# Attention worked by pairs of heads, with products in alternating halves of the array and transposes in rounds

## What is computed

```python
def block_attention(q, k, v):
    ...
    def one(qblk):
        s = jnp.einsum('bkgqd,bksd->bkgqs', qblk, k).astype(jnp.float32) * scale
        p = jax.nn.softmax(s, axis=-1).astype(v.dtype)
        return jnp.einsum('bkgqs,bksd->bkgqd', p, v)
    o = lax.map(one, qb)
    return o.transpose(1, 0, 4, 2, 3, 5).reshape(b, L, H * hd)
```

## Time and profile before

| | |
|---|---|
| median of 3 runs | 2622.45 us (2621.61 to 2622.78) |
| profiled execution | 2621.94 us |
| its span in the trace | 2620.1 us |
| mean granted TensorE clock | 0.965 of full speed |
| PE busy | 2414.7 us (92%) |
| DVE busy | 1489.8 us (57%) |
| ACT busy | 802.6 us (31%) |
| attention loop (first L969 to last L994) | about 1812.8 to 2041.8 us |

### The profile page before, as it was taken

One profiled execution on the slowest core, in us unless ns is written; L12 is line 12 of the kernel. 1 busy time (PEld: TensorE's weight loads), 2 busy tenths in 40 slices (PEclk: granted clock), 3 DMA queues, 4 the chain that ended last, 5 costly groups with the idle time before them and its releaser, 6 DMA issues.

```text
span 2620.1 us, 35077 instructions
## 1 busy us (share of the span) xinstructions
PE 2414.7 (92%) x14569; PEld 2083.2 (80%) x14569; DVE 1489.8 (57%) x2298; ACT 802.6 (31%) x1429; POOL 229.0 (9%) x257
## 2 busy tenths in 40 slices
PE   5899889989998897979999999799999979999998
PEld 3768758878887886769899998687767769989997
DVE  3376571278226865556464555596666466446555
ACT  3423332200221044253122223533444352213222
POOL 0022040033003301010000000200000010000001
PEclk9999999999999998989999999898999989999999
DMA  7401105500450021313222222111000112212221
GB/s 294 145 25 61 65 21 217 201 9 1 169 185 17 1 81 56 105 41 97 65 73 73 73 65 81 55 57 45 1 1 1 41 57 73 65 57 89 77 77 41
DMA packets 43853, 193.57 MB, mean 74 GB/s; under 512 B 5009, under 2 KB 5009, under 8 KB 36913
## 3 DMA queue, kind: packets, MB, share of 16 engines
q1 hardware_dynamic: 41472, 178.10, 20.1%
q0 software_dynamic: 2224, 13.24, 1.4%
HBM read 183.72 MB, written 7.60 MB: 73 GB/s over the span
## 4 chain that ended last, share of the span: by engine, by line
PE 79%; DVE 14%; ACT 3%; issue 2%; DMA 1%; POOL 1%; SPq 0%; DVEq 0%; ACTq 0%; POOLq 0%
PE pg L797 27%; PE pg L593 15%; PE pg L835 15%; PE pg L969 4%; PE ps L744 3%; PE ps L994 3%; PE ps L982 2%; PE ps L567 1%; DVE att L1690 1%; DVE wk L1696 1%; DVE rtb L1443 1%; PE ps L687 1%; DMA ring<-in_wstream 1%; PE ps L691 1%; PE ps L708 1%
## 5 line engine op out<-in xcount | busy, mean ns | idle before, releaser
L797 PE MATMUL pg<-hh,xhi 128*128 128x320 f32 x992 | 312.1, 315 | 25.2 <-DVE hl L1528 25.2
L797 PE MATMUL pg<-hl,xhi 128*128 128x320 f32 x992 | 308.4, 311 | 0.0
L797 PE MATMUL pg<-hh,xlo 128*128 128x320 f32 x992 | 308.1, 311 | 0.0
L1417 DVE TENSOR_TENSOR wlo<-ring,whi 128x1024 fp32r<-128x1024 f32 x129 | 156.9, 1222 | 185.9 <-ACT whi L1030 185.7
L593 PE MATMUL pg<-hh,whi 128*128 128x320 f32 x976 | 239.2, 327 | 23.3 <-DVE hl L1449 10.9
L593 PE MATMUL pg<-hl,whi 128*128 128x320 f32 x976 | 225.6, 313 | 0.0
L593 PE MATMUL pg<-hh,wlo 128*128 128x320 f32 x976 | 225.1, 312 | 0.0
L593 PEld LDWEIGHTS pg<-hh,whi 128*128 128x128 f32 x976 | 165.5, 192 | 62.4 <-issue 51.3
L797 PE MATMUL pg<-hh,whi 128*128 128x320 f32 x640 | 201.5, 315 | 12.9 <-DVE hl L1528 12.9
L797 PEld LDWEIGHTS pg<-hh,xhi 128*128 128x128 f32 x992 | 189.1, 191 | 28.6 <-issue 17.5
L797 PE MATMUL pg<-hl,whi 128*128 128x320 f32 x640 | 199.3, 311 | 0.0
(11 more groups left out here) (296 smaller groups left out, 4762.2 us busy)
## 6 DMA issues: line engine op xcount, KB each, us to landing
ring<-in_wstream SPq DMA_DIRECT2D x231, 512.0 KB, 3.7
adaring<-in_wada SPq DMA_DIRECT2D x21, 1024.0 KB, 5.1
ybuf<-in_wada SPq DMA_DIRECT2D x21, 1024.0 KB, 4.9
adabig<-in_wada SPq DMA_DIRECT2D x6, 1024.0 KB, 17.5
xk<-in_x SPq DMA_DIRECT2D x1, 2560.0 KB, 9.9
yssd_scratch<-ybuf POOLq DMA_DIRECT2D x2, 1280.0 KB, 6.2
xk<-yssd_scratch POOLq DMA_DIRECT2D x1, 2560.0 KB, 10.7
xk<-in_x_tok POOLq DMA_DIRECT2D x1, 2560.0 KB, 9.0
```

What stands on the lines that cost most here:

```text
L797: last = nc.tensor.matmul(out[:, half], w[:, k * P:(k + 1) * P], a[:, k, half * HALF:(half + 1) * HALF], start=k == 0 and m == 0, stop=k = ...
L1417: V.tensor_tensor(lo, flat(ring[:, s % RING]), hi.bitcast(F32), ALU.subtract).then_inc(wlo_ready, 1)
```

## The change

The units become 40 pairs `(hp, b)` (`ATT_PAIRS`): an even and an odd head of one block, 32 full pairs and 8 prompt pairs, every fifth pair being one of the latter.

- Scores of a pair are four products in the order even 512, odd 128, odd 512, even 128 columns, in three banks, the middle one shared; before the last product PE waits on `sc_side` for the second one. Even pairs use three banks of `pg`, odd pairs three of `ps`. The fourth bank of `pg` takes the transposes, the fourth of `ps` the value products of both heads.
- The ten transposes of a full pair go in three rounds of 4, 4 and 2 blocks through that one bank. ACT copies rounds 0 and 1 (512 columns each), DVE copies round 2 (`att_rest`, 256 columns). Each round waits for the copy of the round before it.
- The value products alternate between the two heads, that is between the two column halves of the array. One DVE copy of 128x128 evacuates both.
- DVE takes both maxima in a row, then one negation for both, one reciprocal for both, and two normalizing products. ACT takes two exps per pair.
- `pt` moves to memory that it shares with `hh` and its neighbours; `pr` has four buffers.

In iteration `p` the orders are, PE: transposes `(p-1, round 0)`, scores `p+1`, transposes `(p-1, 1)`, values `p-2`, transposes `(p-1, 2)`. ACT: exp `(p, even)`, copy `(p-1, 0)`, exp `(p, odd)`, copy `(p-1, 1)`. DVE: prob `p-1`, rest `p-2`, max `p+1`, evac `p-2`.

```diff
-ATT_UNITS = [(h, b) for h in range(ATTN_HEADS) for b in range(TT)]
+ATT_PAIRS = [(hp, b) for hp in range(ATTN_HEADS // 2) for b in range(TT)]
+NPAIR = len(ATT_PAIRS)
+def att_rounds(p):
+    if ATT_PAIRS[p][1] == PROMPT_TT:
+        return [[(0, 0), (1, 0)]]
+    blocks = [(par, j) for par in range(2) for j in range(TT)]
+    return [blocks[0:4], blocks[4:8], blocks[8:10]]
+def att_count(p, k=0):
+    full = sum(len(att_rounds(q)) for q in range(p)) + k
+    late = sum(len(att_rounds(q)) == 3 for q in range(p)) + (k > 2)
+    return full, full - late, late
...
+        def scores(p, par):
+            three = (ps if p % 2 else pg)[:].rearrange("p a b -> p (a b)")
+            if ATT_PAIRS[p][1] == PROMPT_TT:
+                return three[:, 1024 * par:1024 * par + P]
+            return three[:, 896:1536] if par else three[:, 0:NT]
+        turn_bank = pg[:, 1, 512:1024]
...
+            def att_scores(p):
+                hp, b = ATT_PAIRS[p]
+                kv = 2 * hp // (ATTN_HEADS // KV_HEADS)
+                if p >= 2:
+                    pe.wait_ge(pe_exp, 2 * (p - 1))
+                def product(par, c0, c1, k0):
+                    r = HD * par
+                    return nc.tensor.matmul(scores(p, par)[:, c0:c1], aq[r:r + HD, hp, b * P:(b + 1) * P],
+                                            ak[r:r + HD, kv, k0:k0 + c1 - c0], start=True, stop=True)
...
+                product(0, 0, SAMPLE, 0)
+                product(1, 0, P, NT).then_inc(sc_side, 1)
+                product(1, P, NT, 0).then_inc(sc_ready, 1)
+                pe.wait_ge(sc_side, 1 + sum(x[1] != PROMPT_TT for x in ATT_PAIRS[:p]))
+                product(0, SAMPLE, NT, NT).then_inc(sc_ready, 1)
+            def att_turn(p, k):
+                rounds = att_rounds(p)
+                if k >= len(rounds):
+                    return
+                pe.wait_ge(pr_ready, 2 * p + rounds[k][-1][0] + 1)
+                _, by_act, by_dve = att_count(p, k)
+                if by_act:
+                    pe.wait_ge(pt_done, by_act)
+                if by_dve:
+                    pe.wait_ge(pt_rest, by_dve)
+                for i, (par, j) in enumerate(rounds[k]):
+                    last = nc.tensor.transpose(turn_bank[:, i * P:(i + 1) * P],
+                                               pr[:, 2 * (p % 2) + par, j * P:(j + 1) * P], cm[:, IDENT, :])
+                last.then_inc(pt_ready, 1)
+            def att_pv(p):
...
+                for j in range(n):
+                    for par in range(2):
+                        v = tiles[par][j]
+                        value = (cvt if v == TT else av[:, v])[:, kv * HD:(kv + 1) * HD]
+                        last = nc.tensor.matmul(ps[HD * par:HD * (par + 1), 3, 0:P], value, pt[:, p % 2, n * par + j, :],
+                                                start=j == 0, stop=j == n - 1, skip_group_check=True)
+            att_scores(0)
+            for p in range(NPAIR + 2):
+                if 1 <= p <= NPAIR:
+                    att_turn(p - 1, 0)
+                if p + 1 < NPAIR:
+                    att_scores(p + 1)
+                if 1 <= p <= NPAIR:
+                    att_turn(p - 1, 1)
+                if p >= 2:
+                    att_pv(p - 2)
+                if 1 <= p <= NPAIR:
+                    att_turn(p - 1, 2)
...
+            def att_exp(p, par):
+                n = P if ATT_PAIRS[p][1] == PROMPT_TT else NT
+                if par == 0:
+                    act.wait_ge(mx_ready, p + 1)
+                    if p >= 2:
+                        act.wait_ge(pt_ready, att_count(p - 1)[0])
...
+            def att_max(p):
+                dve.wait_ge(sc_ready, 2 * (p + 1))
+                for par in range(2):
+                    last = V.reduce_max(mxs[:, p % 2, 0, par:par + 1], scores(p, par), AX_X)
+                link(last)
+                V.tensor_scalar(mxs[:, p % 2, 1], mxs[:, p % 2, 0], -HD ** -0.5, None, ALU.mult).then_inc(mx_ready, 1)
+            def att_prob(p):
+                n = P if ATT_PAIRS[p][1] == PROMPT_TT else NT
+                dve.wait_ge(pe_exp, 2 * (p + 1))
+                link(V.reciprocal(mxs[:, p % 2, 3], mxs[:, p % 2, 2]))
+                for par in range(2):
+                    row = pr[:, 2 * (p % 2) + par, 0:n]
+                    V.tensor_scalar(row, row, mxs[:, p % 2, 3, par:par + 1], None, ALU.mult).then_inc(pr_ready, 1)
+            def att_rest(p):
+                if len(att_rounds(p)) < 3:
+                    return
+                dve.wait_ge(pt_ready, att_count(p, 2)[0] + 1)
+                src, dst = turned_blocks(p, 2)
+                V.tensor_copy(dst, src).then_inc(pt_rest, 1)
+            att_max(0)
+            for p in range(NPAIR + 2):
+                if 1 <= p <= NPAIR:
+                    att_prob(p - 1)
+                if p >= 2:
+                    att_rest(p - 2)
+                if p + 1 < NPAIR:
+                    att_max(p + 1)
+                if p >= 2:
+                    att_evac(p - 2)
```

More of the change, by code:

```diff
@@ L226, in hybrid_step @@
         wlo = sb("wlo", [P, 2, KT, P], F32R)
+        with ExitStack() as ph:
+            pt = sb("pt", [P, 2, 2 * TT, P], F32, ph)
         hh = sb("hh", [P, KT, NT], F32R)
@@ L470, in hybrid_step @@
         pt_done = sem("pt_done")
+        pt_rest = sem("pt_rest")
+        sc_side = sem("sc_side")
         ao_ready = sem("ao_ready")
@@ L955, in _ @@
                 pe.wait_ge(tile_free[b], freed(b, T_AOUT))
-            def keys(b):
-                if b == PROMPT_TT:
[L960 to L983, removed]
-                last.then_inc(pt_ready, 1)
@@ L986, in att_pv @@
[L986 to L1007, removed]
+            def att_scores(p):
[7 more added lines that the diff above has]
+                                            ak[r:r + HD, kv, k0:k0 + c1 - c0], start=True, stop=True)
+                if b == PROMPT_TT:
+                    for par in range(2):
+                        product(par, 0, P, SAMPLE).then_inc(sc_ready, 1)
+                    return
[4 more added lines that the diff above has]
+                product(0, SAMPLE, NT, NT).then_inc(sc_ready, 1)
@@ new lines, in att_pv @@
+            def att_pv(p):
+                hp, b = ATT_PAIRS[p]
+                kv = 2 * hp // (ATTN_HEADS // KV_HEADS)
+                tiles = [[PROMPT_TT]] * 2 if b == PROMPT_TT else [[0, 1, 2, 3, TT], [TT, 0, 1, 2, 3]]
+                n = len(tiles[0])
+                _, by_act, by_dve = att_count(p + 1)
+                pe.wait_ge(pt_done, by_act)
+                if by_dve:
+                    pe.wait_ge(pt_rest, by_dve)
+                if p:
+                    pe.wait_ge(ao_done, p)
+                for j in range(n):
[4 more added lines that the diff above has]
+                                                start=j == 0, stop=j == n - 1, skip_group_check=True)
+                        if j == n - 1:
+                            last.then_inc(ao_ready, 1)
@@ L1371, in _ @@
             nc.scalar.copy(tr_evac_k[1], ps[:, 1, :].rearrange("p (k t) -> p k t", k=KV_HEADS)[:, :, 0:HD]).then_inc(tr_done, 1)
[L1372 to L1394, removed]
+            def att_exp(p, par):
[4 more added lines that the diff above has]
+                        act.wait_ge(pt_ready, att_count(p - 1)[0])
+                nc.scalar.activation(pr[:, 2 * (p % 2) + par, 0:n], scores(p, par), ACT.Exp, scale=HD ** -0.5,
+                                     bias=mxs[:, p % 2, 1, par:par + 1],
+                                     accum_out=mxs[:, p % 2, 2, par:par + 1]).then_inc(pe_exp, 1)
@@ new lines, in att_copy @@
+            def att_copy(p, k):
+                if k >= len(att_rounds(p)):
+                    return
+                act.wait_ge(pt_ready, att_count(p, k)[0] + 1)
+                if p >= 2 and k == 0:
+                    act.wait_ge(ao_ready, 2 * (p - 1))
+                src, dst = turned_blocks(p, k)
+                nc.scalar.copy(dst, src).then_inc(pt_done, 1)
+            for p in range(NPAIR + 1):
+                if p < NPAIR:
+                    att_exp(p, 0)
+                if p:
+                    att_copy(p - 1, 0)
+                if p < NPAIR:
+                    att_exp(p, 1)
+                if p:
+                    att_copy(p - 1, 1)
@@ L1899, in _ @@
             dve.wait_ge(tr_done, 16)
[L1900 to L1913, removed]
```

29 lines of the change are left out of this document (12 added, 17 removed).

## The result

The changed kernel takes 2649.0 us (median of 4 runs, 2647.2 to 2650.8) against 2622.2 before: a ratio of 1.0102, 95% interval 1.0089 to 1.0115. It is 27 us slower where 13 were forecast. The profiled execution took 2650.8 us and has a span of 2649.0 us, 28.9 more than before (that the span equals the median is chance).

The account below looks back on a forecast made before the run. Attention was taken as bound by PE's own instructions, afterwards by a ring through DVE. Eight groups at 234 us, a third at half clock, plus 5 for ends and 3 for start: 242, 13 more than now, 2635 us; range 2606 to 2655.

Parts of the forecast that it names:

- What bounds the kernel now: Attention before the change: bound by PE's own instructions, PE busy for 228.99 of 229.00 us.
- PE's work after the change: Attention: column and row halves overlap, so PE's occupancy per full pair falls from 6.42 to 3.92 us.
- The ring through DVE: Attention turn: PE and DVE wait for each other through rest, transposes, scores, max; 5.96 us per full pair.
- the wait on `sc_side`, costed at nothing: Scores of a full pair: wait ends inside the odd 512-column product, costing nothing; 0.3 us without that cover.
- The forecast of 2635: Whole kernel: 2621.9 + 13 us, with a third of the attention stage at half clock.
- The sizes of the turn: Attention: PE and DVE steps of one full-pair turn at full clock, together 5.96 us against 6.42.
- the group of five: Attention: four full pairs and a prompt one, 26.1 us at full clock against 27.7 before.
- The clock: Attention stage: PE's waits make the granted clock fall, a third at half clock, mean 0.83.
- The rival in which it holds: Attention stage: clock stays up, the 5.96 us turn runs all the way, 2612 us (2604 to 2617); chance 0.27.
- The second rival, row halves in series: Scores: row halves not side by side, 2.34 us a pair; 2648, up to 2670 with falling clock; chance 0.13.
- The range: Whole kernel: 2606 to 2655 us, meant to hold 8 in 10.

Follow-up runs that it names:

- e1: The changed kernel with the odd head's 128-column score product issued first, ahead of the even 512-column one: 2634.2 us.
- e7: The changed kernel with a full pair's score products issued head by head, so row halves do not run side by side: 2742.2 us.
- e2: The changed kernel with PE's scores of pair p+1 issued ahead of transposes (p-1, 0) instead of behind them: 2594.8 us.
- e5: The changed kernel with all 32 full pairs first and the 8 prompt pairs last: 2633.7 us.
- e10: The changed kernel with the edits of both e4 and e1, fillers plus odd 128-column product first: 2615.4 us.
- e4: The changed kernel with five unread 128-column filler products per turn, issued where PE would wait for DVE: 2625.8 us.
- e6: The changed kernel with a pair's value products issued head by head instead of alternating column halves: 2666.7 us.

## Why the prediction was wrong

- **What bounds the kernel now, and PE's work after the change: right.** PE's busy time fell from 229 to 183 us. Column halves overlap as the earlier trace rows said, 1.29 us for 20 passes; row halves overlap too (1.28 us in e1), which no row had shown; e7 shows what they are worth.
- **The ring through DVE: right in place.** In the waits above PE waits for `att_rest` 32 times and DVE for scores, and e2 removes the ring and 54 us with it, some 24 of them by way of the clock. The way of the ring is half right. The prediction took it over DVE's maxima and had the value products end 0.17 us before their evacuation is due (3.64 against 3.81). Measured, the value products of a full pair end after the maxima at full clock too: the chain runs over them at 1870.27 and 1876.31 above and in e5's turns of 6.04 us.
- **The step that failed: the wait on `sc_side`, costed at nothing.** I took it as covered by the odd 512-column product, and wrote that without cover it would cost 0.3 us. It is not covered: the signal of the short product came only when the long one issued before it was done, at 1875.19 against a modelled end of 1874.53. The wait does end while the odd 512-column product is still running, as the prediction says (its last pass had started at 1874.80 and a pass of 512 columns takes 0.43), but with 0.04 us of it left. The even 128-column product, which was to run beside it, ran alone behind it. Scores took 1.61 us instead of 1.27. At full clock that is 10.4 us (e10 against e4), in the change 14.9 (e1), where part of the stage is at half clock. The forecast of 2635 is the time of e1, 2634.2, the kernel with that wait gone; the change is 14.9 above it.
- **The Trainium skill** (TensorE: Matmul & The Clock Gate, Part 3) says that matmuls start and end in program order. I set it aside on the earlier trace rows, which show that passes overlap and say nothing of when a product is signalled as done. Half of it holds here. Starts overtake: in the change the odd head's first product starts with the even one's first pass (1874.04 both), ahead of its second (1874.57). Signals of completion do not, as e1 shows. By that half the wait would have been priced right.
- **The sizes of the turn.** At full clock a turn of full pairs was to be 5.96 us; with the longer scores it is 5.83 or 6.04 (e4, e5), so the rest of it was 0.3 to 0.5 too long: two maxima in a row take 1.56 us, not 1.65, the two normalizing products 1.02, not 1.11. The turn that begins with a prompt pair's maxima was to be about 4.9 us and is 6.34, 6.05 without the `sc_side` wait (e10): I had put its maxima on the ring and missed that the value products of the full pair before it end later. These misses cancel in the group of five, 26.1 us predicted: e10's group takes 26.7, or 26.1 less the fillers' 0.67. That the sum is right is luck.
- **The clock: right, in place and size.** Granted 0.85 in the stage, 0.83 forecast. I had priced it at 23 us (2635 against 2612); e4 takes 23.2 away, which is about 28 less the 5 that its fillers cost. The rival in which it holds is out for the change, and true for e4.
- **The Trainium skill's rule on idle gaps** (TensorE: Matmul & The Clock Gate, "Why this matters for your kernels"), to avoid long idle gaps of PE between bursts of matmuls, would have kept the clock at full. PE's idle stretches in the changed kernel are at most 1.9 us once the stage has started up (one of 3.0 us lies at 1819), and the clock fell to half 14 times after that, from 1837 to 2059. The measurement decides against it.
- **The second rival, row halves in series,** gave 2648 and so nearly the measured time, by a mechanism that is not there: its nearness is luck. The kernel in which it is true, e7, takes 2742, with scores of 2.68 us where the rival had 2.34.

The range held the time, the sign was right, but the loss was twice the forecast's, because one wait was taken as hidden by work that its signal had to wait for.

## What to carry to other kernels

Before an engine's work is cut, write down the ring that the new order closes: which wait stands in front of the work that the other engine is waiting for. Here the same work took 2649, 2595 (two calls exchanged) or 2573 us (three calls and one product moved) by the order of issue on PE alone. The signal of the short product came no earlier than the product issued ahead of it was done, so a product whose completion another one needs belongs first. A TensorE that waits a little in every turn can lose its clock: here waits of at most 1.9 us, one or more per turn, cost some 28 us in that way, by estimate, more than twice the wait on `sc_side`.

## What the runs showed of the hardware

- Products in different row halves, and in different column halves, run side by side at full rate: 1.28 us for a pair's scores (e1; 2.68 head by head, e7), 1.29 for its value products (after). Issued head by head, column halves still overlap in part (1.96 us, e6).
- PE starts products of the other half ahead of their place in the program, but signals them in order: a product whose modelled end is 1874.53 was signalled at 1875.19, after the product issued before it had ended at 1875.16, and so in 32 of 32 pairs. That an engine works its instructions in the order of the program, as the first section has it, does not hold for the starts of PE's passes.
- The granted clock of the stage did not follow PE's busy time: 0.85 with 183.2 of 253.7 us (after), 0.63 with 289.2 of 348.7 (e7, one row half at a time in the scores), 0.98 with 156.6 of 200.0 (e2). Why e7 stays at half clock for so long is open; the kernel before, whose scores also use one row half, ran its stage at full clock once it had come up after 20 us.
- Useless products added to PE (e4, 205.7 us busy in the stage instead of 183.2) made the kernel 23 us faster, though they lengthened turns at full clock by 0.67 us in five.
